# Input rows transposed on arrival and kept in device memory as residual, and weight low parts moved from POOL to DVE up to the first attention tiles

## The reference

```
h  = rmsnorm(x, g_mix);  p = h @ w_in                 # 6672 columns
qA,kA,vA,qB,kB,vB,rb,a1,ga,gb = split(p)
oa = sliding-window attention(qA,kA,vA)               # 16 heads, ALiBi, sinks, 64-frame chunks
ob = gated linear attention(qB,kB,vB, decay from a1)  # 4 heads
m  = sigmoid(ga)*oa + sigmoid(gb)*rmsnorm(ob)*silu(rb)
x2 = x + m @ w_out                                    # x is the residual that the change touches
y  = x2 + (silu(f@w_gate) * (f@w_up)) @ w_down,  f = rmsnorm(x2, g_ffn)
```

## Time and profile before

| | |
|---|---|
| median of the runs | 904.92 us (904.55 to 907.67) |
| profiled execution, its own time | 906.86 us |
| its span in the profile | 905.1 us |
| PE busy | 879.7 us (97%) |
| DVE busy | 581.2 us (64%) |
| ACT busy | 415.7 us (46%) |
| POOL busy | 272.6 us (30%) |
| device memory read, written | 71.45 MB, 3.60 MB |

### The profile page before, as it was taken

One profiled execution on the slowest core, in us unless ns is written; L12 is line 12 of the kernel. 1 busy time (PEld: TensorE's weight loads), 2 busy tenths in 40 slices (PEclk: granted clock), 3 DMA queues, 4 the chain that ended last, 5 costly groups with the idle time before them and its releaser, 6 DMA issues.

```text
span 905.1 us, 17293 instructions
## 1 busy us (share of the span) xinstructions
PE 879.7 (97%) x7077; PEld 850.0 (94%) x7077; DVE 581.2 (64%) x1124; ACT 415.7 (46%) x762; POOL 272.6 (30%) x161
## 2 busy tenths in 40 slices
PE   6999999999999999999999999999999999999998
PEld 5999999999998999898999988999999999999997
DVE  6864656657884445556465889983279853689732
ACT  6633442445445444444435666542155532366421
POOL 2442323232332323323233212235223153222350
PEclk9999999999999999999999999999999999999999
DMA  8331222221422222221117458863288823788322
GB/s 239 111 86 55 82 59 71 59 82 47 116 71 71 54 64 64 56 70 49 48 43 195 108 119 175 184 142 115 62 176 187 163 83 113 157 178 172 93 79 63
DMA packets 154343, 94.17 MB, mean 104 GB/s; under 512 B 5121, under 2 KB 145111, under 8 KB 154263
## 3 DMA queue, kind: packets, MB, share of 16 engines
q1 hardware_dynamic: 139638, 72.74, 28.4%
q0 software_dynamic: 9504, 17.31, 12.2%
q10 hardware_dynamic: 5120, 3.02, 1.2%
HBM read 71.45 MB, written 3.60 MB: 83 GB/s over the span
## 4 chain that ended last, share of the span: by engine, by line
PE 75%; DVE 14%; ACT 4%; DMA 3%; issue 3%; POOL 0%; SPq 0%; DVEq 0%; POOLq 0%
PE G L640 14%; PE G L642 13%; PE G L641 13%; PE G L916 4%; PE G L918 4%; PE G L919 4%; PE X L916 4%; PE X L918 4%; PE X L919 4%; DVE qAT L1663 2%; PE X L833 2%; PE X L817 2%; DMA csum<-csum 2%; PE X L802 2%; DVE rs L1457 1%
## 5 line engine op out<-in xcount | busy, mean ns | idle before, releaser
L640 PE MATMUL G<-h_hi,w_hi 128*128 128x272 f32 x1280 | 382.9, 299 | 5.5 <-DVE rv L1626 2.3
L642 PE MATMUL G<-h_hi,w_lo 128*128 128x272 f32 x1280 | 370.8, 290 | 0.0
L641 PE MATMUL G<-h_lo,w_hi 128*128 128x272 f32 x1280 | 369.3, 289 | 0.0
L582 POOL TENSOR_TENSOR w_lo<-wraw,w_hi 128x1024 fp32r<-128x1024 f32 x84 | 213.9, 2551 | 398.7 <-ACT w_hi L1050 398.6
L640 PEld LDWEIGHTS G<-h_hi,w_hi 128*128 128x128 f32 x1280 | 241.7, 189 | 14.5 <-issue 10.2
L641 PEld LDWEIGHTS G<-h_lo,w_hi 128*128 128x128 f32 x1280 | 241.9, 189 | 0.8
L642 PEld LDWEIGHTS G<-h_hi,w_lo 128*128 128x128 f32 x1280 | 241.5, 189 | 0.0
L1050 ACT ACTIVATE w_hi<-wraw 128x1024 fp32r<-128x1024 f32 (+1 forms) x129 | 134.5, 1045 | 58.7 <-PE G L642 35.2
L1239 ACT ACTIVATE prob<-prob,nm 128x256 f32<-128x256 f32 (+2 forms) x80 | 36.7, 460 | 63.9 <-DVE sd L1695 63.9
L2009 DVE TENSOR_TENSOR rs<-G,rv 128x544 f32<-128x544 f32 x23 | 16.7, 724 | 75.6 <-PE G L642 75.6
L1370 ACT ACTIVATE sq<-sq 128x544 f32<-128x544 f32 x22 | 14.5, 658 | 96.1 <-DVE sq L1896 96.1
(11 more groups left out here) (321 smaller groups left out, 1838.5 us busy)
## 6 DMA issues: line engine op xcount, KB each, us to landing
wraw<-in_w_in_dram SPq DMA_DIRECT2D x52, 512.0 KB
wraw<-in_w_gate_dram SPq DMA_DIRECT2D x22, 512.0 KB
wraw<-in_w_up_dram SPq DMA_DIRECT2D x22, 512.0 KB
csum<-csum POOLq DMA_DIRECT2D x44, 256.0 KB, 4.8
wraw<-in_w_down_dram SPq DMA_DIRECT2D x16, 448.0 KB
wraw<-csum POOLq DMA_DIRECT2D x22, 256.0 KB, 3.5
wraw<-in_w_out_dram SPq DMA_DIRECT2D x8, 512.0 KB
wraw<-in_w_down_dram SPq DMA_DIRECT2D x8, 512.0 KB
```

Source lines behind the costliest of these rows:

```text
L582: pool.tensor_tensor(w_lo[:, slot, :, :], wraw[:, slot, :, :], w_hi[:, slot, :, :].bitcast(F32), ALU.subtract).then_inc(w_split, 1)
L640: pe.matmul(o, w_hi[:, slot, kc, :], b_hi[:, kc, cols], start=(kc == 0), stop=False)
L641: pe.matmul(o, w_hi[:, slot, kc, :], b_lo[:, kc, cols], start=False, stop=False)
L642: mm = pe.matmul(o, w_lo[:, slot, kc, :], b_hi[:, kc, cols], start=False, stop=(kc == last))
```

## The change

- **Raw rows are turned.** Rows arrive in the order samples, 0, 1, 2, 3 (`RAW_ORDER`). PE turns each block as it arrives (`turn_raw`, 8 transposes a block) into X[0], X[1], G[1], X[0] again and a part of G[0]. ACT copies blocks 4, 1, 2 and DVE blocks 0, 3 into `xTr` (`keep_raw`, `RAW_ACT`, `RAW_DVE`). The sums of squares no longer write to PSUM. `keep_busy` falls from 10 and 11 to 4 and 9.
- **They are kept.** SP writes `xTr`, 128 x 8 x 544 numbers, to device memory (`x_turned_dram`, semaphore `xs_out`) after weight tile 3 and w_a2, ahead of the caches and of tile 4. DVE waits for `xs_out` before `gate_sums(0)`, since the scan's output lies over `xTr`. The gate logits wait for w_a2 alone; the caches are waited for at `gla_scores(0)`.
- **They come back.** `residual(i)` loads 128 x 544 numbers straight into `xTi`, now four buffers. `turn_residual`, ACT's copy and `xcol` go.
- **Low parts.** POOL makes those of tiles 0 to 3 and from `HANDOVER` = tile 34 on. DVE makes those of tiles 4 to 33 (`weight_low_part`), tile n + 2 at the head of its loop over n.
- **Memsets.** The six memsets of unused rows (`empty_rows`) move from behind h_lo to DVE's loop, tile 3, because their targets lie over `xTr`.

```diff
+XTS = 4
+RAW_ORDER = (4, 0, 1, 2, 3)
+RAW_ACT, RAW_DVE = (4, 1, 2), (0, 3)
+HANDOVER = UNIT0 + 4
...
@@ sync
-            load_rows(range(NJ))
+            load_rows(RAW_ORDER)
...
                 if n == RING - 1:
                     sp.wait_ge(const_dve, 4)
-                    for dst, src in [(wa2[0:RANK, :], w_a2[0]),
-                                     (wa2[RANK:2 * RANK, :], w_a2[0]),
-                                     (kc_tok[:, :], cache_k[0, 0].rearrange("t h d -> t (h d)")),
+                    for r in range(2):
+                        sp.dma_start(wa2[r * RANK:(r + 1) * RANK, :], w_a2[0]).then_inc(in_wa2, 16)
+                    sp.wait_ge(x_raw_act, len(RAW_ACT))
+                    sp.wait_ge(x_raw_dve, len(RAW_DVE))
+                    sp.dma_start(x_turned_dram, xTr[:, :, :]).then_inc(xs_out, 16)
+                    for dst, src in [(kc_tok[:, :], cache_k[0, 0].rearrange("t h d -> t (h d)")),
...
             def residual(i):
-                if i >= 2:
-                    sp.wait_ge(xt_done, i - 1)
-                c = slice(i * P, (i + 1) * P)
-                sp.dma_start(xcol[:, i % 2, 0:SJ, :], x_prompt[0, :, c].rearrange("(j p) n -> p j n", p=P))\
-                    .then_inc(in_xcol[i % 2], 16)
-                sp.dma_start(xcol[0:DEC, i % 2, SJ, :], x_sample[0, :, c]).then_inc(in_xcol[i % 2], 16)
+                n = OUT0 + i - XTS
+                if i >= XTS:
+                    sp.wait_ge(set_free[n % 2], uses_before(n) + 1)
+                sp.dma_start(xTi[:, i % XTS, :], x_turned_dram[:, i, :]).then_inc(in_xres[i % XTS], 16)
...
@@ gpsimd
-            lows(range(1, GU0[0]))
+            lows(range(1, RING))
+            pool.wait_ge(w_split, HANDOVER)
+            lows(range(HANDOVER, GU0[0]))
...
@@ tensor
+            def turn_raw(j):
+                t0, nt = TOK[j]
+                pe.wait_ge(in_x[j], 16)
+                if j == 3:
+                    pe.wait_ge(x_raw_dve, 1)
+                for c in range(KC):
+                    mm = pe.transpose(RAW[j][:, c * nt:(c + 1) * nt], xtok[0:nt, j, c * P:(c + 1) * P],
+                                      ident[0:nt, 0:nt])
+                mm.then_inc(x_raw, 1)
...
-            keep_busy(G[0][:, 640:640 + P], 10)
+            for j in RAW_ORDER:
+                turn_raw(j)
+            keep_busy(G[0][:, 640:640 + P], 4)
+            pe.wait_ge(x_raw_act, 1)
...
-            keep_busy(X[1][:, 0:P], 11)
+            keep_busy(G[0][:, 640:640 + P], 9)
...
-                    if i == 1 and kc == 2:
-                        turn_residual(0)
-                    if i >= 1 and kc == (6 if i == 1 else 4):
-                        turn_residual(i)
...
@@ scalar
+            def keep_raw(j):
+                t0, nt = TOK[j]
+                act.wait_ge(x_raw, RAW_ORDER.index(j) + 1)
+                act.activation(xTr[:, :, t0:t0 + nt], RAW[j].rearrange("p (c n) -> p c n", c=KC), ACT.Copy)\
+                    .then_inc(x_raw_act, 1)
...
-                act.wait_ge(xt_done, i + 1)
-                if i >= 2:
-                    act.wait_ge(set_free[n % 2], uses_before(n))
-                act.activation(xTi[:, i % 2, :], X[0][:, 0:T], ACT.Copy).then_inc(xt_ok, 1)
...
@@ vector
+                t0, nt = TOK[RAW_DVE[k]]
+                dve.wait_ge(x_raw, RAW_ORDER.index(RAW_DVE[k]) + 1)
+                dve.tensor_copy(xTr[:, :, t0:t0 + nt], RAW[RAW_DVE[k]].rearrange("p (c n) -> p c n", c=KC))\
+                    .then_inc(x_raw_dve, 1)
...
+            def weight_low_part(m):
+                s = m % RING
+                dve.wait_ge(hi_done, m + 1)
+                if m == RING:
+                    dve.wait_ge(w_split, RING)
+                dve.tensor_tensor(w_lo[:, s, :, :], wraw[:, s, :, :], w_hi[:, s, :, :].bitcast(F32),
+                                  ALU.subtract).then_inc(w_split, 1)
...
             for n in range(N_IN):
+                if n == gate_tile(HEADS_B - 1) + 1:
+                    empty_rows()
+                if RING <= n + 2 < HANDOVER:
+                    weight_low_part(n + 2)
...
+                        if h == 0:
+                            dve.wait_ge(xs_out, 16)
                         gate_sums(h)
...
-                dve.wait_ge(xt_ok, i + 1)
-                dve.tensor_tensor(h2(x2T[:, i, :]), halves(G[n % 2]), h2(xTi[:, i % 2, :]), ALU.add)\
+                dve.wait_ge(in_xres[i % XTS], 16 * (i // XTS + 1))
+                dve.tensor_tensor(h2(x2T[:, i, :]), halves(G[n % 2]), h2(xTi[:, i % XTS, :]), ALU.add)\
                     .then_inc(set_free[n % 2], 1)
```

More of the change, by code:

```diff
@@ L51 @@
 RANK = 16
-N_CACHES = 5
+N_CACHES = 3
 TAU = 16.0
@@ L275, in mixer_program @@
         rows = ExitStack()
-        tensor(rows, "gap_gaT", [P, 2 * KC, T])
+        tensor(rows, "gap_gaT", [P, KC, T])
+        xTr = tensor(rows, "xTr", [P, KC, T])
         xtok = tensor(rows, "xtok", [P, NJ, D])
@@ L398, in mixer_program @@
         m_lo_ok = sem("m_lo_ok")
-        xt_done = sem("xt_done")
-        xt_ok = sem("xt_ok")
+        x_raw = sem("x_raw")
+        x_raw_act = sem("x_raw_act")
+        x_raw_dve = sem("x_raw_dve")
+        xs_out = sem("xs_out")
+        in_wa2 = sem("in_wa2")
         x2_sq = sem("x2_sq")
@@ L408, in mixer_program @@
         f01_hi_ok = sem("f01_hi_ok")
-        in_xcol = [sem("in_xcol0"), sem("in_xcol1")]
+        in_xres = [sem(f"in_xres{r}") for r in range(XTS)]
         fin_ok = sem("fin_ok")
@@ L527, in _ @@
             sp.wait_ge(qk_done, NU)
-            residual(0)
-            residual(1)
+            sp.wait_ge(xs_out, 16)
+            for i in range(XTS):
+                residual(i)
             def gate_weights(g, i):
@@ L538, in _ @@
                 if i in (RING + 1, RING + 3):
-                    residual(i // 2)
+                    residual(XTS + i // 2 - 2)
             for i in range(2):
                 gate_weights(0, i)
-                residual(RING + 2 * i)
+                residual(XTS + 2 + i)
                 up_weights(0, i)
-                residual(RING + 2 * i + 1)
             for g, m in enumerate(FF_GROUPS):
@@ L659, in keep_busy @@
                     pe.matmul(ps, ones[:, :], ones[:, :], start=True, stop=True)
+            def turn_raw(j):
[7 more added lines that the diff above has]
+                mm.then_inc(x_raw, 1)
             pe.wait_ge(const_pool, 1)
             pe.wait_ge(const_dve, 1)
-            pe.wait_ge(in_x[1], 16)
-            keep_busy(G[0][:, 640:640 + P], 10)
+            for j in RAW_ORDER:
+                turn_raw(j)
+            keep_busy(G[0][:, 640:640 + P], 4)
+            pe.wait_ge(x_raw_act, 1)
             pe.wait_ge(in_small, 16 * N_SMALL)
             pe.transpose(G[0][:, 0:24], prow[:, :], ident[0:24, 0:24])
-            pe.matmul(G[0][:, 512:512 + HEADS_A], ones[0:1, :], srow[:, :], start=True, stop=True)\
+            pe.matmul(G[0][:, 32:32 + HEADS_A], ones[0:1, :], srow[:, :], start=True, stop=True)\
                 .then_inc(setup_pe, 1)
-            pe.wait_ge(x_sums, len(ROWS_DVE))
-            keep_busy(X[1][:, 0:P], 11)
+            keep_busy(G[0][:, 640:640 + P], 9)
             def turn_input(c):
@@ L677, in turn_input @@
                     pe.wait_ge(x_scaled_dve, len(SCALE_DVE) * (1 + c // (KC // 2)))
-                if c >= 3:
+                if c == 0:
+                    pe.wait_ge(x_raw_dve, 2)
+                elif c < 3:
+                    pe.wait_ge(x_raw_act, c + 1)
+                else:
                     pe.wait_ge(h_ok, c - 2)
@@ L716, in gla_scores @@
                 pe.wait_ge(z_free, HEADS_B)
-                if h >= 1:
+                if h == 0:
+                    pe.wait_ge(in_caches, 16 * N_CACHES)
+                else:
                     pe.wait_ge(gla_norm, h)
@@ L883, in _ @@
                         step(*args)
[L886 to L894, removed]
             for i in range(KC):
@@ L1097, in _ @@
                 act.wait_ge(in_x[j], 16)
-                if k >= 2:
-                    act.wait_ge(x_sq, k - 1)
-                act.activation((G[1], X[0])[k % 2][0:nt, :], xtok[0:nt, j, :], ACT.Square,
+                if k >= 1:
+                    act.wait_ge(x_sq, k)
+                act.activation(sq[0:nt, :, :].rearrange("p a n -> p (a n)")[:, 0:D], xtok[0:nt, j, :], ACT.Square,
                                accum_out=rv[0:nt, j:j + 1]).then_inc(x_sq, 1)
+                if j == SJ:
+                    keep_raw(SJ)
+            keep_raw(1)
+            keep_raw(2)
             act.wait_ge(x_sq, len(ROWS_ACT))
@@ L1107, in _ @@
             act.wait_ge(x_root, 1)
+            act.wait_ge(x_raw, NJ)
             for part in range(2):
@@ L1754, in merged_low_part, with empty_rows @@
                     .then_inc(m_lo_ok, 1)
+            def weight_low_part(m):
[5 more added lines that the diff above has]
+                                  ALU.subtract).then_inc(w_split, 1)
+            def empty_rows():
+                for a, b in ((DEC, 64), (64, P)):
```

(7 more changed lines are left out.)

22 lines of the change are left out of this document (10 added, 12 removed).

## The result

The changed kernel takes 896.98 us (median of 4 runs, 896.3 to 897.51) beside 905.27 for the kernel before on the same chip (904.55 to 907.67): 0.9902 of it, 95% interval 0.9887 to 0.9917. The forecast was 901.5; the time lies at the low end of the range, where the rival "relief wins" stood (896.9). Profiled, the execution took 897.51 us with a span of 895.5, against 906.86 and 905.1.

What follows compares the result with a forecast made beforehand. PE, busy 879.7 of 905.1 us, was taken as the bound. Start +0.9, first gate head +0.9, tiles 7 to 33 +0.1 and output projection -5.3 sum to -3.4: 904.92 to 901.5 us, range 896.5 to 906.5.

Steps and rivals of the forecast that it cites:

- relief wins: Rival, chance 0.25: with POOL silent, PE's waits for DVE shrink and a slow-clock stretch goes; -8.0 us, to 896.9.
- What bounds the kernel: Whole kernel: PE is busy 879.7 of 905.1 us, so only PE work or PE's waits count.
- Start, +0.9: Up to the first turned h: DVE's added PSUM copy of block 3 delays the root; +0.9 us, bounds -0.3 to +3.5.
- Cold start: Rival at the start, chance 0.10: clock stays at 1.2 GHz until the keep-busy matmuls; +3.5 for 0.9, 904.1 us.
- First gate head, +0.9: Tiles 3 to 5: memsets and low parts delay DVE, less POOL blocking recovers some; +0.9 us, bounds 0 to +3.3.
- Tiles 7 to 33, +0.1: Middle input tiles: less POOL blocking against added low parts; 0.3 - 0.8 + 0.6 = +0.1 us, bounds -5 to +3.
- No PE wait hangs on: Seven blocked qA tiles: each loses 2.1 us and gains 1.2 on DVE, with no effect on PE.
- "+0.6" at 278.8: PE's 1.90 us wait for the second attention unit's maxima: low part 33 and POOL's tile 34 lengthen it by 0.6.
- the first 1.16 wait: PE's mean-square wait at 175.61: unblocking saves 0.8 us, but head 3's masks hand it back, leaving +0.3.
- Output projection, -5.3: Output tiles: removing turn_residual takes 6.3 us off PE, DVE's lateness returns 0.9; -5.3 us, bounds -6.3 to -2.7.
- FFN, 0: FFN after the output projection: later waits move along with PE, so no term of its own; 0.
- the slow end of the forecast: Write of the turned rows: at 218 GB/s it takes 10.2 us and delays by 2.4.

Runs made afterwards that it cites:

- e6: Changed kernel with DVE's low parts only up to tile 20, POOL making the later ones; 900.26 us, 0.9944 of the kernel before.
- e4: Changed kernel with DVE's low part at the end of its loop body and the memsets behind the wait for the write; 901.18 us, 0.9947.
- e5: Changed kernel with DVE's low part after the attention slot, ahead of gates and norms, and memsets behind the wait for the write; 894.34 us, 0.9871.
- e8: Changed kernel without both keep_busy calls; 898.53 us, 0.992 of the kernel before.
- e2: Changed kernel with all low parts of the input weights on POOL again; 900.0 us, 0.9938 of the kernel before.
- e1: Kernel before with only the low parts of tiles 4 to 33 moved to DVE; 901.27 us, 0.9943 of the kernel before.
- e10: e5 run again without any edit, in another call; 896.0 us, 0.9884 of the kernel before.
- e7: Changed kernel with DVE making the low parts of all input tiles up to 52; 903.12 us, 0.997 of the kernel before.
- e3: Changed kernel with POOL also making the low parts of tiles 4 to 33, which DVE then makes again; 920.76 us, 1.0161 of the kernel before.

## Why the prediction missed, point by point

- **What bounds the kernel: right.** All that moved the time was PE work, PE's waits, or PE's clock.
- **Start, +0.9: mis-sized, +0.13.** Order and copy were as described. The copy ended at 11.96 and not at 12.6, since the last block arrived 0.4 earlier than taken and the copy began 1.15 behind the start of the sum and not 1.37. Beside the kernel before the copy costs next to nothing: it fills the 1.15 in which DVE waited for ACT's part of the root, and the refinement starts at 11.87 in place of 11.74. "Cold start" is refuted by the 0.14 us transposes at 9.60.
- **First gate head, +0.9: right in its steps, with the clock left out; +2.04.** Tile 5 starts at 56.33 (56.4 forecast) after a wait of 1.86 (1.7 forecast), and the 1.17 wait is gone. The write delays tile 4's load, so that its high part starts at 28.32 (25.87 before) and the first gate logs at 29.29 (28.53 before, 29.9 forecast), but PE's shift is still +0.16 at 46. A stretch of 3.4 us at half clock follows the wait and costs 1.5. e6, the same kernel up to there, has the same wait without that stretch, and there the head costs +0.6. The working priced just such a stretch behind 278.8 and did not ask whether the wait that it created itself might bring one. That e4 and e5, which shorten the wait, have no stretch there proves nothing, since e6 and e8 keep the wait and have none either.
- **Tiles 7 to 33, +0.1: the step that failed, -4.96.** Three terms of it. "No PE wait hangs on" the qA tiles: -1.4, since DVE's cycle of 7.27 was their pitch; e6 gives it back. "+0.6" at 278.8: -1.0, which e6 gives back too. The block of the maximum came as forecast (1.08 at L1716), but DVE came to it 1.2 earlier than before (275.86 in place of 277.03); that the shorter qA tiles are the reason is argued, not tested by itself. The slow clock behind it, left standing in the forecast: -1.5. This term is partly chance: e2 and e6 keep the wait of 1.9 and have no slow clock behind it. The other terms held: the first 1.16 wait was handed back to the masks (-1.0, then +0.8), the second stayed (-0.9, forecast -0.8).
- **Output projection, -5.3: right, a little small, -6.0.** 8 x 0.80 = 6.4 off PE as reckoned; DVE was late by 0.2 and not by 0.9. Part of that is a slip in the working: its four figures for DVE sum to 24.9, which from 497.0 gives 521.9 for the last fb, not 522.3. e2 shows -5.9 without the low parts.
- **FFN, 0: -0.84, open.** Waits for c_lo in two groups are shorter, 0.24 and 0.88 where 0.55 and 1.58 stood. Ahead of the second, one of POOL's accumulating DMAs (wraw<-csum, issued at 771.4) landed in 4.5 us in place of 5.2; the medians of these DMAs hardly moved or rose (wraw<-csum 3.5 to 3.4, csum<-csum 4.8 to 5.2). e2 has the gain as well (-1.46) and e1 has not (-0.03), which points to the residual's part; e5 and e10, one kernel, differ by less than 0.1 there, but whether the change does it was not tried.
- **"Relief wins" met the time partly by cancelling.** The waits went as it said. It did not have the qA tiles (-1.4), nor the masks (+0.8) and the clock behind tile 5 (+1.5), and its start was 0.8 too dear.

By the traces the two parts hinder each other in the first head: the residual brings the memsets ahead of tile 4, the low parts stand ahead of vB. With the low parts alone (e1) the vB wait is 0.7 and the clock stays full.

## What to carry to other kernels

Before writing that no wait of the bounding engine hangs on a stage, compare the stage's pitch with the busy cycle of each other engine: one that idles only for its own helper sets the pitch, even where the bounding engine's waits look like nothing. When an edit creates or removes a wait of nearly 2 us on PE, a stretch at half clock behind it (1.5 us here) may come or go with it: carry it as a chance and not as a fixed term, and before a microsecond between two profiles is called a gain, look whether one of them merely lacks such a stretch. Work that holds a port which two engines share should start behind the other engine's short critical operations; a blocked 0.16 us operation cost 1.7 us here, and one added wait on POOL took that back.

## What the runs showed of the hardware

- Transposes alone raise TensorE's clock from 1.2 to 2.4 GHz: 0.23 us each in the set at 5.04, 0.14 at 9.60, and the same in e8 without any keep-busy matmul. The Trainium skill (TensorE: Matmul & The Clock Gate, Part 4: PE-mode transpose) says that full clock does not engage in transpose mode; for this kernel's f32 transposes, which the trace lists as MATMUL without saying in which mode they ran, these runs decide against it. The granted clock of the record is no help before its first change, since it prints 1.00 for the slow set too:

```profile
5.00:8.50 3.50, 3.46 (x16) 3.46 (x17) 2.06 (x3) 1.40 (x3) 0.00 (x0) 1.00 1.03 364
8.70:10.50 1.80, 1.80 (x17) 1.71 (x16) 1.03 (x2) 1.80 (x4) 0.00 (x0) 1.00 0.09 13
```

- A wait of 1.8 to 1.9 us on PE is followed by a stretch of about 3.4 us at half clock, which costs some 1.5 us, in some executions only. In these profiles it was in five cases (before at 278.8; changed kernel and e7 at 56.3; e4 at 104.5 and 143.0) and was not in four (e2 at 279.1; e6 at 56.3 and 278.7; e8 at 56.9). The five longer ones, 2.3 to 3.6 us (e3 at 53.8, 181.3, 222.3 and 297.5; e8 at 13.8), all had one; those of 1.56 to 1.57 (e4, e5, e10) had none. The 1.3 and 1.8 of the first FFN pair brought one in e3, e5, e6 and e10 and none in the other eight profiles. What decides was not tried.
- The same shows in the repeats of the kernel before: of its 32 executions beside the experiments five were granted 0.999 or more of the clock, and these took 904.0 to 904.6 us; the other 27 took 905.0 to 908.5.
- The write of 2176 KB landed 9.8 us after its issue, 227 GB/s and so near the slow end of the forecast, and cost PE nothing. The v cache behind it took 9.3 in place of 3.9, and tile 4's high part started 2.4 us later than before.
